# Gathering the tokens of two experts with one set of 256-column products, in a loop over four pairs

## The reference

```python
def swiglu(h, w_in, w_out):
    g, u = jnp.split(jnp.einsum('bld,df->blf', h, w_in), 2, axis=-1)
    return jnp.einsum('blf,fd->bld', jax.nn.silu(g) * u, w_out)

def moe_swiglu(h, w_router, w_exp_in, w_exp_out):
    logits = jnp.einsum('bld,de->ble', h, w_router).astype(jnp.float32)
    top_v, top_i = lax.top_k(logits, TOP_K)
    gates = jax.nn.softmax(top_v, axis=-1)
    dense_gate = jnp.sum(jax.nn.one_hot(top_i, N_EXPERTS, dtype=jnp.float32) * gates[..., None], axis=-2)
    y = jnp.zeros_like(h)
    for e in range(N_EXPERTS):
        y = y + dense_gate[..., e:e + 1] * swiglu(h, w_exp_in[e], w_exp_out[e])
    return y
```

## Time and profile before

| | before |
|---|---|
| median of 3 runs | 1978.37 us (1975.26 to 1980.34) |
| profiled execution, its time / its span | 1978.76 us / 1977.0 us |
| layer 0, mixer 1 and routing | the first 927 us of the span |
| expert loop | 927 to 1948 us |
| last scatters and final norm | 1948 us to the end |
| TensorE busy | 1854.8 us (94%), 9997 matmuls |
| VectorE busy / ScalarE busy | 1346.6 us (68%) / 1046.3 us (53%) |
| memory read | 440.14 MB |

### The profile page before, as it was taken

One profiled execution on the slowest core, in us unless ns is written; L12 is line 12 of the kernel. 1 busy time (PEld: TensorE's weight loads), 2 busy tenths in 40 slices (PEclk: granted clock), 3 DMA queues, 4 the chain that ended last, 5 costly groups with the idle time before them and its releaser, 6 DMA issues.

```text
span 1977.0 us, 25921 instructions
## 1 busy us (share of the span) xinstructions
PE 1854.8 (94%) x9997; PEld 1609.8 (81%) x9997; DVE 1346.6 (68%) x1177; ACT 1046.3 (53%) x913; POOL 76.0 (4%) x85
## 2 busy tenths in 40 slices
PE   6998988998989989977999999999999999999995
PEld 5987877998979978765888888888888888888884
DVE  3636544444346355545988889889898898888986
ACT  3443223333233333223677767776777767677674
POOL 2002120000000021300000000000000000000000
PEclk9998869999989979787999999999999999999997
DMA  7432143443452521142999999999999999999992
GB/s 238 149 109 57 35 115 104 150 150 110 124 173 89 168 51 35 42 160 69 340 361 331 351 339 346 363 328 355 363 321 355 333 353 363 322 357 342 344 352 98
DMA packets 267757, 452.11 MB, mean 229 GB/s; under 512 B 41242, under 2 KB 102930, under 8 KB 267688
## 3 DMA queue, kind: packets, MB, share of 16 engines
q1 hardware_dynamic: 265824, 447.51, 65.6%
q0 software_dynamic: 1600, 3.46, 0.8%
q10 hardware_dynamic: 264, 0.17, 0.1%
HBM read 440.14 MB, written 10.97 MB: 228 GB/s over the span
## 4 chain that ended last, share of the span: by engine, by line
PE 89%; DVE 7%; ACT 2%; issue 1%; DMA 0%; POOL 0%; DVEq 0%; SPq 0%; ACTq 0%
PE ps L1473 16%; PE ps L1474 16%; PE ps L1999 10%; PE ps L1468 7%; PE ps L1469 7%; PE ps L2014 5%; PE ps L1547 3%; PE ps L1913 3%; PE ps L1654 2%; PE ps L1639 2%; DVE cvt L1018 1%; PE ps L1928 1%; PE ps L2042 1%; PE ps L1809 1%; DVE spL L916 1%
## 5 line engine op out<-in xcount | busy, mean ns | idle before, releaser
L1364 DVE TENSOR_TENSOR spL<-ring,spH 128x2048 fp32r<-128x2048 f32 x339 | 771.8, 2291 | 115.7 <-ACT spH L847 115.6
L847 ACT ACTIVATE spH<-ring 128x2048 fp32r<-128x2048 f32 x339 | 648.5, 1916 | 134.2 <-PE ps L2014 72.8
L1473 PE MATMUL ps<-spH,XH 128*128 128x512 f32 x896 | 357.6, 399 | 1.5 <-DVE XL L1376 1.5
L1474 PE MATMUL ps<-spH,XL 128*128 128x512 f32 x896 | 352.3, 393 | 0.0
L916 DVE TENSOR_TENSOR spL<-ring,spH 128x2048 fp32r<-128x2048 f32 (+1 forms) x74 | 158.3, 2146 | 236.8 <-ACT spH L572 236.7
L1468 PE MATMUL ps<-hnH,spH 128*128 128x320 f32 x928 | 276.0, 312 | 13.7 <-DVE hnL L934 7.1
L1469 PE MATMUL ps<-hnL,spH 128*128 128x320 f32 x928 | 274.4, 310 | 0.0
L572 ACT ACTIVATE spH<-ring 128x2048 fp32r<-128x2048 f32 (+1 forms) x74 | 132.7, 1798 | 246.0 <-PE ps L1547 108.3
L1999 PE MATMUL ps<-spL,XH 128*128 128x512 f32 x896 | 242.4, 392 | 0.0
L1473 PEld LDWEIGHTS ps<-spH,XH 128*128 128x128 f32 x896 | 169.0, 189 | 38.4 <-issue 1.7
L1999 PEld LDWEIGHTS ps<-spL,XH 128*128 128x128 f32 x896 | 168.8, 188 | 37.4
(11 more groups left out here) (321 smaller groups left out, 2118.7 us busy)
## 6 DMA issues: line engine op xcount, KB each, us to landing
ring<-in_w_exp_in_dram SPq DMA_DIRECT2D x227, 1024.0 KB, 7.3
ring<-in_w_exp_out_dram SPq DMA_DIRECT2D x112, 1024.0 KB, 7.1
ring<-in_w_in_dram SPq DMA_DIRECT2D x28, 1024.0 KB, 5.9
ring<-in_w_ffn_in_dram SPq DMA_DIRECT2D x22, 1024.0 KB, 5.2
ring<-in_w_ffn_out_dram SPq DMA_DIRECT2D x16, 704.0 KB, 4.6
ring<-in_w_out_dram SPq DMA_DIRECT2D x8, 1024.0 KB, 5.2
out_dram<-ring SPq DMA_DIRECT2D x32, 256.0 KB, 2.6
ring<-in_state_hgrn_dram SPq DMA_DIRECT2D x16, 256.0 KB, 3.8
```

The lines of the kernel that those rows point to most:

```text
L847: A(esplit(j)[0], src, ACT.Copy).then_inc(S("hi_done"), 1)
L1364: V.tensor_tensor(lo, eslot(j)[0], hi.bitcast(F32), ALU.subtract).then_inc(S("split_done"), 1)
L1473: mm(out, x[0], w, start=start, stop=False)
L1474: return mm(out, x[1], w, start=False, stop=False)
```

## The change

Experts are taken in pairs: the loop has four iterations, and each body holds the 42 units of expert `x = 0` and then those of `x = 1`. `sel`, `XH` and `XL` are twice as wide (256 columns, 128 for each expert). One gather serves the next pair: 8 tiles of channels x 5 matmuls of 256 columns. Its sums need four banks, filled in the order 2, 3, 0, 1; it stands behind up unit 37 of the second expert, and before the third bank it waits for the product of chunk 6 (`late`). The splits of the gathered tokens are four pieces of 128 x 512 per pair where there were two per expert. `sel` is written once per pair, six instructions instead of three, and the first one ahead of the loop is six too. Scatter, turning, weight loads and the sync engine's loop over eight experts stay as they are; the semaphore counts are renumbered.

```diff
-        sel = put("sel", [P, 3, P], F32R)
+        sel = put("sel", [P, 3, 2 * P], F32R)
...
-        XH = put("XH", [P, KT, P], F32R, offset=base + 4 * KT * TOK)
-        XL = put("XL", [P, KT, P], F32R, offset=base + 8 * KT * TOK)
+        XH = put("XH", [P, KT, 2 * P], F32R, offset=base + 4 * KT * TOK)
+        XL = put("XL", [P, KT, 2 * P], F32R, offset=base + 8 * KT * TOK)
...
-                for q in range(2):
-                    act.wait_ge(S("gath_mm"), it * 2 + (q + 1))
-                    A(XH[:, 4 * q:4 * q + 4],
-                      ps[:, 2 + q, :].rearrange("p (k n) -> p k n", k=4), ACT.Copy).then_inc(S("X_done"), 1)
+                for q in range(4):
+                    act.wait_ge(S("gath_mm"), it * 4 + (q + 1))
+                    A(XH[:, 2 * q:2 * q + 2], ps[:, (q + 2) % 4, :].rearrange("p (k n) -> p k n", k=2), ACT.Copy
+                      ).then_inc(S("X_done"), 1)
...
-                for p in range(EU):
+                for x, p in itertools.product(range(2), range(EU)):
+                    j = x * EU + p
...
-                    if p == UP_LAST[-1]:
+                    if j == EU + UP_LAST[-1]:
                         gathered(it + 1)
...
-            with act.Fori(0, NE) as e:
-                expert_act(e)
+            with act.Fori(0, NE // 2) as e:
+                pair_act(e)
...
+            def one_hot(ranks):
+
+                for x in range(2):
+                    for t in range(3):
+                        i = V.tensor_scalar(sel[:, t, x * P:(x + 1) * P], tabv("iota"), ranks[:, x, t:t + 1], None,
+                                            ALU.is_equal)
+                i.then_inc(S("sel_done"), 1)
...
-            def gather(it):
+            def gather(it, late=None):
 
                 pe.wait_ge(S("sel_done"), it + 1)
-                for q in range(2):
-                    for k in range(4):
-                        kk = 4 * q + k
-                        out, d = ps[:, 2 + q, k * P:(k + 1) * P], slice(kk * P, (kk + 1) * P)
+                for q in range(4):
+                    if q == 2 and late:
+                        pe.wait_ge(late[0], late[1])
+                    for k in range(2):
+                        kk = 2 * q + k
+                        out, d = ps[:, (q + 2) % 4, k * 2 * P:(k + 1) * 2 * P], slice(kk * P, (kk + 1) * P)
                         for t in range(2):
                             mm(out, hkH[:, t, d], sel[:, t], start=t == 0, stop=False)
                             mm(out, hkL[:, t, d], sel[:, t], start=False, stop=False)
...
-                    if j == UP_LAST[-1]:
-
-                        pe.wait_ge(S("eh_done"), it * EC + EC)
-                        gather(it + 1)
+                    if u == EU + UP_LAST[-1]:
+
+                        pe.wait_ge(S("eh_done"), it * (2 * EC) + 2 * EC)
+                        gather(it + 1, (S("eh_done"), it * (2 * EC) + (2 * EC + 1)))
...
-            with pe.Fori(0, NE) as e:
-                expert_pe(e)
+            with pe.Fori(0, NE // 2) as e:
+                pair_pe(e)
```

More of the change, by code:

```diff
@@ L888, in _ @@
                 with act.Fori(1, rounds) as r:
-                    with act.Fori(0, NE) as e:
-                        expert_act(act.snap(r * NE + e))
+                    with act.Fori(0, NE // 2) as e:
+                        pair_act(act.snap(r * (NE // 2) + e))
             tables(LN_EXP)
@@ L1361, in expert_lo @@
             def expert_lo(it, j):
-                dve.wait_ge(S("hi_done"), it * EU + (U0 + j + 1))
+                dve.wait_ge(S("hi_done"), it * PAIR + (U0 + j + 1))
                 hi, lo = esplit(j)
                 V.tensor_tensor(lo, eslot(j)[0], hi.bitcast(F32), ALU.subtract).then_inc(S("split_done"), 1)
[L1366 to L1370, removed]
@@ L1372, in gathered_lo @@
             def gathered_lo(it):
[L1374 to L1379, removed]
+                for q in range(4):
+                    dve.wait_ge(S("X_done"), it * 4 + (q + 1))
+                    V.tensor_tensor(XL[:, 2 * q:2 * q + 2], ps[:, (q + 2) % 4, :].rearrange("p (k n) -> p k n", k=2),
+                                    XH[:, 2 * q:2 * q + 2].bitcast(F32), ALU.subtract).then_inc(S("XL_done"), 1)
@@ L1386, in scatter_add, with pair_dve @@
                                        op0=ALU.mult, op1=ALU.add).then_inc(S("ht_add"), 1)
-            def expert_dve(e, it):
-                nxt = dve.snap(e + 1)
-                for p in range(EU):
+            def pair_dve(e, it):
+                nxt = dve.snap(e * 2 + 2)
+                for x, p in itertools.product(range(2), range(EU)):
+                    j = x * EU + p
                     if p == SELT_AT + 1:
-                        dve.wait_ge(S("selT_tr"), it + 1)
+                        dve.wait_ge(S("selT_tr"), it * 2 + (x + 1))
@@ L1430, in _ @@
             gathered_lo(0)
-            with dve.Fori(0, NE) as e:
-                expert_dve(e, e)
+            with dve.Fori(0, NE // 2) as e:
+                pair_dve(e, e)
             rounds = dve.value_load(rndi[0:1, 0:1], min_val=1, max_val=MAXR)
@@ L1437, in _ @@
                     dve.drain()
[L1438 to L1441, removed]
+                    with dve.Fori(0, NE // 2) as e:
+                        pair_dve(e, dve.snap(r * (NE // 2) + e))
+            last = dve.snap(rounds * (NE // 2))
+            dve.wait_ge(S("rk_done"), last * 3 + 1)
             for b in range(6):
-                scatter_add(last, b, 2 + b)
+                scatter_add(last, 0, b, 2 + b)
             dve.drain().then_inc(S("moe_sum"), 1)
@@ L2050, in _ @@
                 with pe.Fori(1, rounds) as r:
-                    with pe.Fori(0, NE) as e:
-                        expert_pe(pe.snap(r * NE + e))
-            done = pe.snap(rounds * NE)
-            pe.wait_ge(S("yL_done"), done * 2 + 2)
+                    with pe.Fori(0, NE // 2) as e:
+                        pair_pe(pe.snap(r * (NE // 2) + e))
+            done = pe.snap(rounds * (NE // 2))
+            pe.wait_ge(S("yL_done"), done * 4 + 2)
             for b in range(6):
```

113 lines of the change are left out of this document (60 added, 53 removed).

## The result

The changed kernel takes 1956.28 us (median of 4 runs, 1946.05 to 1963.06) where the kernel before takes 1978.62 us (4 runs, 1975.26 to 1980.34): a ratio of 0.9891, with a 95% interval from 0.9863 to 0.9919. The prediction was 1969, with a range from 1963 to 1977. The kernel is faster, as forecast, and by about twice as much as forecast.

What follows compares the result with a forecast made beforehand. TensorE's issue was taken to bound the expert loop. From 1978.76 us, -15.3 for gathers, +0.55 for `sel` ahead of the loop and +5.1 for three branches back gave -9.6, so 1969 us, range 1963 to 1977.

Steps and rivals of the forecast that it cites:

- the main term: Gathers in the loop: a pair's gathering falls from 8.82 to 5.0 us, saving 15.3 us over four pairs.
- the clock at the first gather: Ahead of the loop: the first gather stays at half clock, 0.213 us per 256-column matmul, its length unchanged.
- the price of the branch back: TensorE's loop end: code must be fetched, a gap of 1.7 us at each of three branches, 5.1 us in all.
- The stop behind the 20th matmul: Mid-gather, before the third bank: a wait for chunk 6's product, 0.2 us per pair, between 0 and 0.5.
- the loads are not the bound: Weight loads in the loop: 1.5% more rate needed, with room; the rival that they bind lies inside a 5% chance.
- The rival of dear 256-column matmuls: Gather: weight loads don't hide, 0.17 us per matmul, 2 us more per pair, total 1977 us; chance 7%.
- the rival of a body that is held: TensorE's loop end: the longer body needs no fetch, branches stay at 0.22 us, total 1964 us; chance 17%.
- Half of these 2.1 added gives 4.4: Branch back: the idle 3.36 us plus half the 2.1 us by which busy DMA engines slow a 1 MB load.
- the idle case: The forward jump over code for further rounds: a fetch with idle DMA engines, 3.36 us, giving a 0.65 us gap.
- the 3.03 us less 0.3: Branch back: 3.03 us until the next weight load hide the branch, less 0.3 us to issue behind it.
- the rival of a dear branch: Loop end: fetch queues behind loads, 9.4 us, gap 6.7, total 1984 us, chance 5%; gaps of 3 to 6 us, 13%.
- the 1.9 us behind it stay: Between first gather and first up unit: the last piece split is as large as before, so 1.9 us remain.

Runs made afterwards that it cites:

- narrow_gather: The changed kernel with each 256-column gather matmul cut into two of 128 columns; 1986.82 us, ratio 1.0043 to the kernel before.
- split_192_64: The changed kernel with each 256-column gather matmul cut into one of 192 and one of 64 columns; 1981.25 us, one run.
- the repeat: The changed kernel run again unchanged, with more rounds, against the kernel before; 1958.47 us, ratio 0.9909.
- after: The changed kernel itself in its first comparison and profile, against the kernel before; 1956.28 us, ratio 0.9891.
- pe_body_two: The kernel before with two experts in TensorE's loop body, work and order unchanged; 1980.16 us, ratio 1.0000.
- warm_first: The changed kernel with 14 unused 512-column matmuls added in TensorE's idle time ahead of the first gather; 1961.08 us, ratio 0.9913.
- shifted_tiles: The kernel before with `sel`, `rank` and `rk` enlarged, moving later tiles to their places in the changed kernel; 1978.69 us, one run.

## Why the prediction was wrong

The direction and the mechanism of the main term held, the size of the gain did not: -19.7 us in the profiles against -9.6, which from the 1978.76 us of the profile before gives 1959, still under the range. Two steps of the prediction failed. One is the clock at the first gather, taken as given where the new instructions changed it (3.8 us). The other is the price of the branch back (5.1 us forecast, 2.1 measured). Closer matmuls, of which the prediction had nothing, are the third part (about 2.5 us). Any one of them put right leaves the sum inside the range (1965 to 1967); it took them together to leave it.

- **The gathers** were right. 0.120 us per matmul and 4.85 to 4.87 us in place of 5.0, so -15.8 instead of -15.3. The stop behind the 20th matmul was 0.09 us, not 0.2. No unit waits for `hTL` or `XL` in the loop, and the loads are not the bound. The first expert of a pair takes 122.7 us (said 122.9), the second 127.4 without the gap behind it (said 128); what is missing to the forecast there are the closer matmuls. The rival of dear 256-column matmuls fell, and narrow_gather with split_192_64 shows why: up to 192 columns there is a floor per matmul, not a price per column.
- **The branch back**: that a fetch comes, with about 30 more pieces on the code queue, was right (37 more); the rival of a body that is held fell. What was mis-sized is the term "three branches, 5.1 us": they cost 2.1, and 1.9 in the repeat. The step "Half of these 2.1 added gives 4.4" failed: the branch took 3.3 to 4.0 us, mean 3.65 in after, next to the 3.36 of the idle case. The gap is the branch less 2.94 to 2.98 us of work already handed on, in all six branches of the two profiles (2.8 to 3.0 in pe_body_two), so the 3.03 us less 0.3 that the prediction allowed were close to right, and a little low. Of the Trainium skill (Runtime: NRT & Kernel Launch, Instruction fetch mechanics), the size of 2048 instructions agrees with this trace: 1,234 are held, 2,384 are not. Slower branches do exist (5.33 us in pe_body_two), and behind that gap the clock also fell; but the rival of a dear branch began at gaps of 3 us, and 2.53 is the longest in any run here.
- **The first gather** is the step whose mechanism failed: "That gather runs at half clock [...] so its length stays", and "the 1.9 us behind it stay". It did begin at half clock. But the prediction took the clock as given, and the changed instructions themselves brought full clock about 10 us earlier. The gather took 6.5 us instead of 8.35, and the first up unit came 1.3 us earlier; more it could not be, since VectorE then ends last (warm_first). And the first expert ran at full clock from its start: -2.5 us, of which the prediction had nothing. narrow_gather shows that it was the wide matmuls: with 80 of 128 columns at this place it cost 9.8 us, and the first expert 2.9 more than in after. split_192_64 repeats it (9.7 and 2.7).
- **Not in the prediction at all**: about 2.5 us of closer matmuls, of which about two thirds come from the moved tiles (shifted_tiles).
- `sel` ahead of the loop cost 0.59 us, said 0.55.

Summed against the prediction: -0.5 for the gathers, -3.0 for the branches, -1.3 and -2.5 for the clock, -2.5 for the tiles, -0.4 behind the loop make -10.2, and -19.7 is 10.1 below -9.6. Between the 1959 that this gives and the measured 1956.28 lie some 3 us; no profile was taken of the median execution, but the end of the routing alone lay between 905 and 916 us in the profiles here.

The range was too narrow for a reason that can be named: it held the bounds of the branch and nothing for terms that I had set to zero. That all of those were gains is chance.

## What to carry to other kernels

Before costing a matmul by its columns, look for the floor: where each brings new weights, narrow ones can be merged at hardly any cost (128 to 256 columns for 0.009 us here), and splitting them is dear. A stretch at half clock is not a constant of the place: when its instructions change, price it once with the clock kept and once with it risen, and look at which other engine then ends last. A loop body that outgrows the held code costs a fetch at each branch back, but what counts is that less the work already handed on, here 3.65 less 2.94 us on the mean; writing the four turns out took the gaps away, though nearly as much code was still brought.

## What the runs showed of the hardware

- At half clock, 40 and even 80 matmuls of 128 columns, one each 0.213 us, went by without a return to full clock (lower level for 23.9 and 34.1 us); 80 of 192 and 64 columns did too (34.1 us); with 256-column ones, also 0.213 us each, it came within the gather (13.7 us).
- Behind a TensorE gap of 2.53 us in the loop the clock fell to its lower level for 3.4 us (1.5 us lost, seen once); behind gaps up to 1.22 us (narrow_gather) it did not.
- A matmul with new weights took 0.111 us from start to start at full clock with 64, 128 or 192 columns, 0.120 with 256 and 0.230 with 512.
- Branches back over 2,384 instructions took 3.3 to 4.0 us (six in the two profiles of the changed kernel), over 1,234 some 0.22; written out, the same work drew 80 pieces of code without a gap.
- The mean distance of equal 512-column matmuls moved from 0.2308 to 0.2305 us when nothing but the place of tiles (and the distance between the parts of `sel`) moved.
- The same code ahead of the first gather ended up to 11 us apart in profiles of kernels with the same tiles (905.30 in split_192_64 to 916.03 us in narrow_gather at the routing's end), which is more than half of this change's gain.
